# Rotary exchange of a head's halves: ScalarE copies between partitions instead of a permutation product

## The chip, the cores and the metric

The kernel runs on one core of one Trainium2 chip. The metric is the device time of one execution in microseconds (us). Names used below: PE is TensorE's matmul, PEld its weight load, DVE VectorE, ACT ScalarE, POOL GpSimd, SP SyncE, which issues most DMAs.

## The reference

Two stacks of layers on 256 tokens of width 1024, all in float32. The first has a recurrent mixer, an attention and two feed-forward layers. The second begins with a projection into q, k, v of two attentions (`m` and `d`) and their gates; q and k get a rotary embedding; then come the attentions, the output product, the routing and 32 experts. Cut to the part at stake:

```python
def apply_rope(x, cos, sin):
    xf = x.astype(jnp.float32)
    half = x.shape[-1] // 2
    x1, x2 = xf[..., :half], xf[..., half:]
    return jnp.concatenate([x1 * cos - x2 * sin, x2 * cos + x1 * sin], axis=-1).astype(x.dtype)

q_m, k_m, v_m, q_d, k_d, v_d, gate_m, gate_d = jnp.split(proj, IN_SPLITS, axis=-1)
qm = apply_rope(to_heads(q_m, MOBA_HEADS, MOBA_HEAD_DIM), cos_m, sin_m)
km = apply_rope(to_heads(k_m, MOBA_HEADS, MOBA_HEAD_DIM), cos_m, sin_m)
qd = apply_rope(to_heads(q_d, 2 * DIFF_HEADS, DIFF_HEAD_DIM), cos_d, sin_d)
kd = apply_rope(to_heads(k_d, 2 * DIFF_HEADS, DIFF_HEAD_DIM), cos_d, sin_d)
```

## The kernel before

Features lie on partitions and tokens along the free axis, so that a head of 64 features is 64 partitions and a tile of 128 partitions holds two heads. The exchange of a head's halves is therefore a movement between partitions: 0-31 with 32-63, 64-95 with 96-127.

**Stages.** Each engine runs a program of its own, written in order by hand; semaphores join them. The stage at stake starts when the feed-forward of the second layer ends and lasts until the attention scores. The weights come in units of 2 MB, named qm, km, vm, qd, kd, vd, gm0 and so on, through three places in SBUF (`RING`). Each product is made of three float32r products of a high and a low part of both operands. For every unit, ACT rounds the weights to the high part in two halves (`hi_unit`, line 715) and DVE subtracts to get the low part in two halves (`lo_unit`, line 1097); PE waits for both parts (`wait_parts`) before the unit's first tile.

**Tiles.** PE makes each unit in two tiles (km0, km1, ...), each in a PSUM bank: `product_pair_parts` (line 1766), `product_pair_rows` for km0 (line 1778), `token_major_parts` for the v units (line 1787). Banks 0 to 3 go round by the order of the list `TILES`; `start_tile` waits until the tile four places earlier has been read out (`evac`). ACT reads a finished tile out with `copy_pair` (line 694). The q of `m` is made apart (`qm_product`, line 2007) and finished in SBUF by `qm_shifted`.

**Rotation.** `rotate` (line 2028) multiplies the tile in SBUF with a 128x128 matrix `rot` of -1 and 1, plain float32, in 4 places of PE's program: for qm behind tile km0, for km behind vm0, for qd behind kd0, for kd behind vd0. Each place has two tiles rot0 to rot7 of two products. DVE then does, for each of the eight (r = 0 to 7), x * cos (line 1417), the exchanged x from PSUM * sin (line 1418), both in two pieces of 256 columns, and their sum (line 1421). In DVE's program, `lo_unit` of qd stands ahead of r = 2, kd behind r = 3, vd ahead of r = 4, gm0 behind r = 7.

**After it.** `pair_scores(0)` (lines 2059, 2062) waits for all eight rotated tiles and for the last read-outs; then come gate products (`gate_tile`, line 2076), the softmax on DVE (from line 1440) and ACT, and later the experts, whose weights SP loads as PE frees the places.

Of the kernel before, what the change touches and what calls it, by code (L numbers as in the profile page):

```python
# [25 lines left out]
P = 128  # L26
# [26 lines left out]
C_ID, C_AFTER, C_BEFORE, C_ONES, C_ROT, C_STICK, C_NEG = 0, 128, 256, 384, 512, 640, 1024  # L53
C_IOTA = 1408
# [31 lines left out]
         + ["km0", "rot0", "rot1", "km1", "vm0", "rot2", "rot3", "vm1",  # L86
            "qd0", "qd1", "kd0", "rot4", "rot5", "kd1", "vd0", "rot6", "rot7", "vd1"]
# [40 lines left out]
def program(nc, a, mod_dram, out):  # L128
    with ExitStack() as ctx:
# [41 lines left out]
        rot = cst[:, C_ROT:C_ROT + P]  # L171
# [49 lines left out]
        rope_u = flat(TMP + 1024, 512)  # L221
        ada_place = [wbuf[:, at:at + UNIT // 2].rearrange("p (j f) -> p j f", j=ADA_GROUP) for at in (6 * MATRIX + UNIT, 6 * MATRIX + UNIT + UNIT // 2)]
# [62 lines left out]
        def col(row, table=0):  # L285
# [28 lines left out]
        ffn_g, ffn_gu, ffn_silu, ffn_hid, ffn_hid_hi, ffn_hid_lo = (  # L314
            sem(n) for n in ("ffn_g", "ffn_gu", "ffn_silu", "ffn_hid", "ffn_hid_hi", "ffn_hid_lo"))
# [13 lines left out]
        mean_ready = sem("mean_ready")  # L329
        merged_ready = sem("merged_ready")  # L330
# [175 lines left out]
        def _(sp):  # L506
# [43 lines left out]
            sp.dma_start(cst[:, C_ROT:], a["constants"][:, C_ROT:]).then_inc(const_in, 16)  # L550
# [119 lines left out]
        def _(act):  # L670
# [166 lines left out]

            act.add_instruction(mybir.InstLoadActFuncSet(name=nc.get_next_instruction_name(), act_func_set_id=EXP_LN_TABLE, ins=[], outs=[]))
# [71 lines left out]
            copy_pair("km0", km[:, 0:2])  # L910
            copy_pair("km1", km[:, 2:4])
# [145 lines left out]
        def _(dve):  # L1057
# [212 lines left out]
            def ffn(layer):  # L1270
# [7 lines left out]
                def step(s, n, following=True):  # L1278
# [12 lines left out]
                    dve.wait_ge(ffn_hid, 2 * n + 1)  # L1291
                    dve.wait_ge(ffn_silu, n + 1)
                    nc.vector.tensor_tensor(hid[:, s], hid[:, s], up_scaled, ALU.mult).then_inc(ffn_hid, 1)
                    dve.wait_ge(ffn_hid, 2 * n + 2)
                    nc.vector.tensor_copy(hid_part[s][0], hid[:, s]).then_inc(ffn_hid_hi, 1)
                    subtract(hid_part[s][1], hid[:, s], hid_part[s][0], ffn_hid_hi, n + 1, ffn_hid_lo)
# [110 lines left out]
            for i, x in enumerate((qm, km, qd, kd)):  # L1407
# [314 lines left out]
        def _(pe):  # L1722
# [288 lines left out]
            def second_product(nm, h):  # L2011
# [4 lines left out]
                else:  # L2016
                    product_pair_parts(f"{nm}{h}", unit_parts(nm), 2 * h, KC, x_part)

            def rotate(nm, x, r):

                for d in range(2):
                    if nm == "qm":
# [349 lines left out]
```

## Time and profile before

| what | value |
|---|---|
| time, median of 3 runs | 1292.6 us (1289.51 to 1292.88) |
| the profiled execution's own time | 1292.79 us |
| its span in the trace | 1291.0 us |
| PE busy | 1120.0 us, 87% |
| DVE busy | 685.0 us, 53% |
| ACT busy | 420.7 us, 33% |
| granted TensorE clock, mean | 0.952 |

The span is the time from the first to the last instruction in the trace; the 1.8 us between it and the execution's time lie around it. Shares of busy time are means over stages with different limits, so the stretch from 636 to 715 us is read by itself: the chain of waits says what the end hung on, the timelines of PE, ACT and DVE say when each started what, and the brackets behind a row how long the engine had been idle and who ended that.

### The profile page before, as it was taken

How to read it: one execution, taken by the hardware profiler on the slowest of the kernel's cores; microseconds unless marked ns; L12 is line 12 of the kernel's file. 1: busy time of each engine (PE TensorE's matmuls, PEld its weight loads, DVE VectorE, ACT ScalarE, POOL GpSimd, SP SyncE). 2: the span in 40 equal slices, each digit the busy share in tenths (PEclk: the TensorE clock that was granted, in tenths of full speed). 3: DMA queues.
4: the chain of work that ended last, by engine and by line, in shares of the span. 5: the costliest groups of instructions: out<-in, count | busy, mean ns of one | idle time of the engine just before them, and what ended most of it. 6: DMA issues, size and time to landing. Idle time of an engine off the chain costs nothing.

```text
span 1291.0 us, 23141 instructions
## 1 busy us (share of the span) xinstructions
PE 1120.0 (87%) x9332; PEld 907.3 (70%) x9333; DVE 685.0 (53%) x1069; ACT 420.7 (33%) x532; POOL 32.7 (3%) x71
## 2 busy tenths in 40 slices
PE   9999999999989999999999999768666667666666
PEld 9999999999968999999998899633232223222222
DVE  5799888887444565556866777532211212112114
ACT  3775333345474333335644673320000000000001
POOL 0000000000000000001000000000000000000000
PEclk9999999999999999999999998899988889888889
DMA  9678988865520965551463335889999999999996
GB/s 349 218 272 303 326 304 302 305 239 189 175 94 1 350 208 170 166 180 34 156 244 131 131 139 210 328 330 409 428 429 429 427 429 428 428 428 429 429 427 255
DMA packets 99401, 362.48 MB, mean 281 GB/s; under 512 B 4160, under 2 KB 51664, under 8 KB 84112
## 3 DMA queue, kind: packets, MB, share of 16 engines
q1 hardware_dynamic: 95216, 335.06, 67.3%
q0 software_dynamic: 3984, 26.50, 5.2%
q8 instruction: 43, 0.70, 0.2%
q14 instruction: 14, 0.11, 0.0%
q10 hardware_dynamic: 144, 0.10, 0.0%
HBM read 360.58 MB, written 1.06 MB: 280 GB/s over the span
## 4 chain that ended last, share of the span: by engine, by line
PE 58%; DMA 24%; DVE 11%; ACT 3%; issue 3%; SPq 1%; POOLq 0%; DVEq 0%; POOL 0%; ACTq 0%
DMA wbuf<-in_w_up 22%; PE ps L1880 16%; PE ps L1803 9%; PE ps L1766 8%; PE ps L2200 6%; DVE parts L1097 3%; PE ps L1787 3%; PE ps L2076 3%; PE ps L1812 2%; PE ps L2220 1%; PE ps L2250 1%; DMA wbuf<-in_ffn_w_in 1%; PE ps L1756 1%; PE ps L1963 1%; DVE wbuf L1175 1%
## 5 line engine op out<-in xcount | busy, mean ns | idle before, releaser
L2200 PE MATMUL ps<-wbuf,big 128*32 128x256 f32 x2176 | 164.6, 467 | 112.4 <-DMA wbuf<-in_w_up 98.4
L1880 PE MATMUL ps<-big_parts,parts 128*128 128x256 f32 x2112 | 257.7, 283 | 4.8 <-DVE parts L1097 4.8
L1880 PEld LDWEIGHTS ps<-big_parts,parts 128*128 128x128 f32 x2112 | 254.9, 190 | 5.8 <-DVE parts L1097 5.8
L1097 DVE TENSOR_TENSOR parts<-wbuf,parts 128x2048 fp32r<-128x2048 f32 x92 | 208.8, 2287 | 88.6 <-ACT parts L829 45.2
L2200 PEld LDWEIGHTS ps<-wbuf,big 128*32 128x32 f32 x2176 | 83.6, 133 | 206.9 <-issue 105.3
L1676 DVE TENSOR_TENSOR big<-big,ps 128x128 f32<-128x128 f32 x33 | 9.5, 288 | 266.5 <-ACT big L1029 266.5
L1029 ACT ACTIVATE big<-ps 128x128 f32<-128x128 f32 x33 | 9.1, 277 | 417.0 <-PE ps L2200 417.0
L1803 PE MATMUL ps<-big_parts,parts 128*128 128x256 f32 x1152 | 142.0, 282 | 1.7 <-DVE parts_f L1347 1.1
L1803 PEld LDWEIGHTS ps<-big_parts,parts 128*128 128x128 f32 x1152 | 139.3, 189 | 2.1 <-issue 1.3
L1766 PE MATMUL ps<-parts_f,parts 128*128 128x256 f32 x704 | 98.4, 284 | 0.0
L1766 PEld LDWEIGHTS ps<-parts_f,parts 128*128 128x128 f32 x704 | 90.5, 192 | 0.1
L2250 PE MATMUL ps<-wbuf,big 128*32 128x512 f32 x544 | 65.4, 596 | 16.2 <-DVE big L1664 16.2
L1097 DVE TENSOR_TENSOR parts<-wbuf,parts_f 128x2048 fp32r<-128x2048 f32 x28 | 63.3, 2288 | 17.7 <-ACT parts_f L715 17.6
L2220 PE MATMUL ps<-big 64*128 64x512 f32 x272 | 67.6, 615 | 2.6 <-DVE big L1672 2.6
L734 ACT ACTIVATE parts<-wbuf 128x2048 fp32r<-128x2048 f32 x22 | 42.1, 1916 | 83.6 <-PE ps L1880 60.0
L715 ACT ACTIVATE parts<-wbuf 128x2048 fp32r<-128x2048 f32 x26 | 48.4, 1905 | 33.1 <-PE ps L1766 18.1
L829 ACT ACTIVATE parts<-wbuf 128x2048 fp32r<-128x2048 f32 x20 | 38.3, 1913 | 63.9 <-PE ps L1803 63.9
L1175 DVE SCALAR_TENSOR_TENSOR wbuf<-wbuf,big 128x1024 f32<-128x1024 f32 x48 | 56.0, 1220 | 0.3 <-DMA wbuf<-in_w_ada 0.3
L737 ACT ACTIVATE parts<-wbuf 128x2048 fp32r<-128x2048 f32 x22 | 42.2, 1916 | 40.5 <-PE ps L1880 36.6
L715 ACT ACTIVATE parts_f<-wbuf 128x2048 fp32r<-128x2048 f32 x28 | 52.4, 1903 | 3.3 <-PE ps L1766 3.3
L2076 PE MATMUL ps<-parts_f 128*128 128x256 f32 x256 | 47.1, 286 | 1.3 <-DVE parts L1097 1.3
L2220 PEld LDWEIGHTS ps<-big 64*128 64x128 f32 x272 | 23.4, 186 | 34.1 <-issue 32.4
(349 smaller groups left out, 1397.8 us busy)
## 6 DMA issues: line engine op xcount, KB each, us to landing
wbuf<-in_w_down SPq DMA_DIRECT2D x32, 2048.0 KB, 37.9
wbuf<-in_w_gate SPq DMA_DIRECT2D x31, 2048.0 KB, 32.6
wbuf<-in_w_up SPq DMA_DIRECT2D x31, 2048.0 KB, 37.1
wbuf<-in_ffn_w_in SPq DMA_DIRECT2D x44, 1024.0 KB, 11.7
wbuf<-in_w_ada POOLq DMA_DIRECT2D x24, 1024.0 KB, 8.6
wbuf<-in_ffn_w_out SPq DMA_DIRECT2D x22, 1024.0 KB, 5.1
wbuf<-in_w_in SPq DMA_DIRECT2D x10, 2048.0 KB, 8.2
wbuf<-in_attn_w_qkv SPq DMA_DIRECT2D x6, 2048.0 KB, 8.6
```

The lines of the kernel that those rows point to most:

```text
L715: nc.scalar.activation(halves(unit_parts(name)[0])[i], halves(unit_view(name))[i], ACT.Copy).then_inc(w_hi, 1)
L734: nc.scalar.activation(fg_part[0], ffn_views(slot)[0], ACT.Copy).then_inc(fg_hi, 1)
L737: nc.scalar.activation(fu_part[0], ffn_views(slot)[1], ACT.Copy).then_inc(fu_hi, 1)
L1097: nc.vector.tensor_tensor(lo, whole, hi.bitcast(F32), ALU.subtract).then_inc(done, 1)
L1175: ins = nc.vector.scalar_tensor_tensor(out=w, in0=w, scalar=1.0, in1=c_row, op0=ALU.mult, op1=ALU.mult, accum_out=ada[:, at:at + 1])
L1766: ins = mm(b[:, d * 256:(d + 1) * 256], w[pw][:, k, (m + d) * P:(m + d + 1) * P], rhs[px][:, k], start=(k == 0 and i == 0), stop=(k == kn ...
L1803: ins = mm(ps[:, 4 + f // 2, (f % 2) * 256:(f % 2 + 1) * 256], w[:, k, f * P:(f + 1) * P], r, start=(first and k == 0 and f % 2 == 0), sto ...
L1880: ins = mm(ps[:, b, d * 256:(d + 1) * 256], w[pw][:, k, d * P:(d + 1) * P], h_part_of[px][:, k], start=(k == 0 and d == 0 and i == 0), sto ...
L2076: ins = mm(ps[:, c % 2, d * 256:(d + 1) * 256], w[pw][:, k, m * P:(m + 1) * P], x_part[px][:, k], start=(k == 0 and i == 0), stop=(k == KC ...
L2200: ins = mm(at, rows, gu_place[s][:, :, k, r * P:(r + 1) * P], start=(k == 0), stop=(k == KC - 1))
L2220: ins = mm(ps[:, 4 + 2 * c + h, :], comb[q][rows, c * P:(c + 1) * P], yE[q][rows, :], start=False, stop=stop, skip_group_check=True)
L2250: ins = mm(ps[r * WIN:(r + 1) * WIN, 2, :], hidT[:, f * WIN:(f + 1) * WIN], d_place[s][:, f, h * 512:(h + 1) * 512], start=(i == 0), stop= ...
```

## The change

The product with `rot` goes, with its matrix in the constants (905 columns loaded become 777) and the tiles rot0 to rot7. In its place ACT copies each quarter of 32 partitions to its partner's place, 4 copies of 32x512 for each of the 8 pairs of tiles' columns, into one of two SBUF buffers `swapped`; the sign moves into the sine table. DVE now works on 512 columns at once, three operations for each r. A semaphore of the feed-forward is merged with its neighbour (same waits; a register operation more in each turn of a loop of four turns, twice).

```diff
-         + ["km0", "rot0", "rot1", "km1", "vm0", "rot2", "rot3", "vm1",
-            "qd0", "qd1", "kd0", "rot4", "rot5", "kd1", "vd0", "rot6", "rot7", "vd1"]
+         + [f"{nm}{i}" for nm in ("km", "vm", "qd", "kd", "vd") for i in range(2)]
...
+        swapped = [flat(WORK + 6144 + 512 * i, 512).rearrange("p (k t) -> p k t", k=2) for i in range(2)]
...
+            def swap_halves(r, of):
+
+                if r >= 2:
+                    act.wait_ge(roped, r - 1)
+                for h in range(P // HD):
+                    for to, at in ((0, HD // 2), (HD // 2, 0)):
+                        ins = nc.scalar.activation(swapped[r % 2][h * HD + to:h * HD + to + HD // 2], of[h * HD + at:h * HD + at + HD // 2], ACT.Copy)
+                ins.then_inc(swap_done, 1)
+
+            def copy_swapped(name, dst, r):
+                wait_tile(act, name)
+                swap_halves(r, bank(name).rearrange("p (k t) -> p k t", k=2))
+                copy_pair(name, dst)
...
             hi_unit("vm")
-            copy_pair("km0", km[:, 0:2])
-            copy_pair("km1", km[:, 2:4])
+            for h in range(2):
+                act.wait_ge(qm_kept, 2 * h + 2)
+                swap_halves(h, qm[:, 2 * h:2 * h + 2])
+            copy_swapped("km0", km[:, 0:2], 2)
+            copy_swapped("km1", km[:, 2:4], 3)
             hi_unit("qd")
             copy_pair("vm0", vm[:, 0])
             copy_pair("vm1", vm[:, 1])
             hi_unit("kd")
-            copy_pair("qd0", qd[:, 0:2])
-            copy_pair("qd1", qd[:, 2:4])
+            copy_swapped("qd0", qd[:, 0:2], 4)
+            copy_swapped("qd1", qd[:, 2:4], 5)
             hi_unit("vd")
-            copy_pair("kd0", kd[:, 0:2])
-            copy_pair("kd1", kd[:, 2:4])
+            copy_swapped("kd0", kd[:, 0:2], 6)
+            copy_swapped("kd1", kd[:, 2:4], 7)
             hi_unit("gm0")
...
-                    wait_tile(dve, f"rot{r}")
-                    for kk in range(2):
-                        nc.vector.tensor_tensor(t3[:, kk], xx[:, kk], rope[:, 0:256], ALU.mult)
-                        ins = nc.vector.tensor_tensor(u3[:, kk], bank(f"rot{r}")[:, kk * 256:(kk + 1) * 256], rope[:, 256:512], ALU.mult)
-                    ins.then_inc(evac_sem(f"rot{r}"), 1)
-                    wait_evac(dve, f"rot{r}")
+                    if nm == "qm":
+                        dve.wait_ge(qm_kept, 2 * d + 2)
+                    else:
+                        wait_evac(dve, f"{nm}{d}")
+                    nc.vector.tensor_tensor(t3, xx, cosine, ALU.mult)
+                    dve.wait_ge(swap_done, r + 1)
+                    link(nc.vector.tensor_tensor(u3, swapped[r % 2], sine, ALU.mult))
                     ins = nc.vector.tensor_tensor(xx, t3, u3, ALU.add)
...
             product_pair_rows("km0", unit_parts("km"), 0, KC, x_part, FH_MOD)
-            rotate("qm", qm, 0)
             second_product("km", 1)
             second_product("vm", 0)
-            rotate("km", km, 2)
             second_product("vm", 1)
             for h in range(2):
                 second_product("qd", h)
             second_product("kd", 0)
-            rotate("qd", qd, 4)
             second_product("kd", 1)
             second_product("vd", 0)
-            rotate("kd", kd, 6)
             second_product("vd", 1)
```

ACT's program before, from the high part of vm on: the read-outs of km (line 694) stand between the high parts of vm and of qd.

```order
L715 ACTIVATE parts_f<-wbuf 128x2048 [waits fu_lo,a_loaded0]
L715 ACTIVATE parts_f<-wbuf 128x2048
L694 ACTIVATE big<-ps 128x512 [waits tile_done] x2
L715 ACTIVATE parts_f<-wbuf 128x2048 [waits tile_done,a_loaded1]
L715 ACTIVATE parts_f<-wbuf 128x2048
```

The same place now, where line 844 is the copy of a quarter:

```order
L715 ACTIVATE parts_f<-wbuf 128x2048 [waits fu_lo,a_loaded0]
L715 ACTIVATE parts_f<-wbuf 128x2048
L844 ACTIVATE big<-big 32x512 [waits qm_kept]
L844 ACTIVATE big<-big 32x512 x3
L844 ACTIVATE big<-big 32x512 [waits qm_kept]
L844 ACTIVATE big<-big 32x512 x3
L844 ACTIVATE big<-ps 32x512 [waits roped,tile_done]
L844 ACTIVATE big<-ps 32x512 x3
L694 ACTIVATE big<-ps 128x512 [waits tile_done]
L844 ACTIVATE big<-ps 32x512 [waits roped,tile_done]
L844 ACTIVATE big<-ps 32x512 x3
L694 ACTIVATE big<-ps 128x512 [waits tile_done]
L715 ACTIVATE parts_f<-wbuf 128x2048 [waits tile_done,a_loaded1]
```

Sixteen copies stand between the two high parts, and eight of them wait for DVE's rotated tiles (`roped`).

PE's program before, at the end of tile km0 (line 1778) and the start of km1 (line 1766):

```order
L1778 MATMUL ps<-parts_f,parts 128x256
L2028 MATMUL ps<-big,cst 128x256 [waits evac1,qm_kept]
L2028 MATMUL ps<-big,cst 128x256
L2028 MATMUL ps<-big,cst 128x256 [waits evac2,qm_kept]
L2028 MATMUL ps<-big,cst 128x256
L1766 MATMUL ps<-parts_f 128x256 [waits evac3]
```

The same place now, where the lines are 1797 and 1785:

```order
L1797 MATMUL ps<-parts_f 128x256 x2
L1797 MATMUL ps<-parts_f,parts 128x256
L1785 MATMUL ps<-parts_f 128x256 [waits evac1]
L1785 MATMUL ps<-parts_f 128x256
```

The four products are gone and km1 goes into bank 1 instead of 3; the other three places change in the same way.

DVE's program now, from the low part of vm (line 1114, before 1097) to that of qd; lines 1437, 1439 and 1440 are the two multiplications and the sum:

```order
L1114 TENSOR_TENSOR parts<-wbuf,parts_f 128x2048 [waits w_hi] x2
L1437 TENSOR_TENSOR big<-big 128x512 [waits qm_kept,rope_in]
L1439 TENSOR_TENSOR big<-big 128x512 [waits swap_done]
L1440 TENSOR_TENSOR big<-big 128x512 [waits dve_ch]
L1437 TENSOR_TENSOR big<-big 128x512 [waits qm_kept,roped]
L1114 TENSOR_TENSOR parts<-wbuf,parts_f 128x2048 [waits w_hi,roped]
```

Every r is now three operations, and the second waits for ACT (`swap_done`) where the first waited for PE's tile.

## Rows read from the trace of the kernel before

**Rows 1.** The page's head: span and instructions

```profile
span 1291.0 us, 23141 instructions
```

**Rows 2.** Chain of waits, 590 to 740 us: start us, us, what

```profile
638.12 1.73 PE ps L2028 x8
...
645.60 5.47 PE ps L1787 x24
...
658.24 17.27 PE ps L1766 x144
...
688.46 0.88 PE ps L2028 x4
...
698.79 0.57 DVE big L1440
...
714.51 6.01 PE ps L2076 x48
```

**Rows 3.** PE's timeline: start us, us, engine, line, shapes, count [idle before <-releaser]

```profile
645.43 0.63 PE L1787 MATMUL ps<-parts_f 128*128 128x512 f32 x2
...
658.08 0.40 PE L1766 MATMUL ps<-parts_f 128*128 128x256 f32 x2
...
696.42 0.49 PE L2059 MATMUL ps<-big 64*128 64x128 f32 x4 [0.78 <-ACT big L694]
...
698.36 0.51 PE L2076 MATMUL ps<-parts_f 128*128 128x256 f32 x2 [1.01 <-DVE parts L1097]
...
714.51 0.50 PE L2076 MATMUL ps<-parts_f 128*128 128x256 f32 x2 [0.26 <-DVE parts L1097]
```

**Rows 4.** ACT's timeline, 605 to 725 us

```profile
638.46 3.70 ACT L715 ACTIVATE parts_f<-wbuf 128x2048 fp32r<-128x2048 f32 x2
642.07 0.57 ACT L694 ACTIVATE big<-ps 128x512 f32<-128x512 f32 x1
...
658.28 0.60 ACT L694 ACTIVATE big<-ps 128x512 f32<-128x512 f32 x1 [6.58 <-PE ps L1787]
658.77 3.71 ACT L715 ACTIVATE parts_f<-wbuf 128x2048 fp32r<-128x2048 f32 x2
```

**Rows 5.** DVE's timeline, 605 to 725 us

```profile
608.87 0.69 DVE L1293 TENSOR_TENSOR big<-big 128x512 f32<-128x512 f32 x1
...
640.55 4.49 DVE L1097 TENSOR_TENSOR parts<-wbuf,parts_f 128x2048 fp32r<-128x2048 f32 x2
644.96 0.41 DVE L1417 TENSOR_TENSOR big<-big 128x256 f32<-128x256 f32 x1
...
646.41 0.69 DVE L1421 TENSOR_TENSOR big<-big 128x512 f32<-128x512 f32 x1
647.13 0.43 DVE L1417 TENSOR_TENSOR big<-big 128x256 f32<-128x256 f32 x1
...
660.78 4.49 DVE L1097 TENSOR_TENSOR parts<-wbuf,parts_f 128x2048 fp32r<-128x2048 f32 x2 [2.72 <-ACT parts_f L715]
```

**Rows 6.** ACT's groups by form: busy us, mean ns | idle before

```profile
L798 ACT ACTIVATE big<-xT 128x512 f32<-128x512 f32 x16 | 9.9, 616 | 0.0
L1029 ACT ACTIVATE big<-ps 128x128 f32<-128x128 f32 x33 | 9.1, 277 | 417.0 <-PE ps L2200 417.0
...
L694 ACT ACTIVATE big<-ps 128x512 f32<-128x512 f32 x10 | 5.9, 595 | 33.9 <-PE ps L1766 18.2 <-PE ps L1787 15.7
```

**Rows 7.** PE's timeline behind four waits

```profile
453.06 13.25 PE L1880 MATMUL ps<-big_parts,parts 128*128 128x256 f32 x96 [2.85 <-DVE parts L1097]
...
919.51 3.66 PE L2200 MATMUL ps<-wbuf,big 128*32 128x256 f32 x64 [2.64 <-DMA wbuf<-in_w_up]
...
948.90 5.35 PE L2200 MATMUL ps<-wbuf,big 128*32 128x256 f32 x64 [4.00 <-DMA wbuf<-in_w_up]
...
1227.83 3.66 PE L2200 MATMUL ps<-wbuf,big 128*32 128x256 f32 x64 [3.58 <-DMA wbuf<-in_w_up]
```

**Rows 8.** Stretches: us, PE busy (x), granted clock, DMA share, GB/s

```profile
454.00:457.80 3.80, 3.80 (x22) 0.56 0.48 153
...
949.00:952.50 3.50, 3.50 (x40) 0.55 1.01 431
```

**Rows 9.** Waits of SP's queue: us in total, times, longest

```profile
SPq L497 <- PE ps L2200: 234.4, 27, 20.7
...
SPq L594 <- DVE info L1646: 22.6, 1, 22.6
```

More of the change, by code:

```diff
@@ L313, in program @@
         ffn_gate_scaled = sem("ffn_gate_scaled")
-        ffn_g, ffn_gu, ffn_silu, ffn_hid, ffn_hid_hi, ffn_hid_lo = (
-            sem(n) for n in ("ffn_g", "ffn_gu", "ffn_silu", "ffn_hid", "ffn_hid_hi", "ffn_hid_lo"))
+        ffn_g, ffn_gu, ffn_silu, ffn_hid, ffn_hid_lo = (
+            sem(n) for n in ("ffn_g", "ffn_gu", "ffn_silu", "ffn_hid", "ffn_hid_lo"))
         fh_hi, fh_lo, fg_hi, fg_lo, fu_hi, fu_lo, fd_hi, fd_lo = (
@@ L549, in _ @@
             sp.dma_start(cst[:, 0:C_ONES], a["constants"][:, 0:C_ONES]).then_inc(const_in, 16)
[L550 removed]
+            sp.dma_start(cst[:, C_STICK:], a["constants"][:, C_STICK:]).then_inc(const_in, 16)
             sp.dma_start(bias36[:], a["rows"][:, 0:N_GRP + N_EXP].to_broadcast([P, N_GRP + N_EXP])).then_inc(lam_in, 16)
@@ L1406, in _ @@
             dve.wait_ge(rope_in, 16)
-            for i, x in enumerate((qm, km, qd, kd)):
+            cosine, sine = (rope[:, SEQ * i:SEQ * (i + 1)].unsqueeze(1).to_broadcast([P, 2, SEQ]) for i in range(2))
+            for i, (nm, x) in enumerate((("qm", qm), ("km", km), ("qd", qd), ("kd", kd))):
                 for d in range(2):
@@ L2017, in second_product @@
                     product_pair_parts(f"{nm}{h}", unit_parts(nm), 2 * h, KC, x_part)
-            def rotate(nm, x, r):
-                for d in range(2):
-                    if nm == "qm":
-                        pe.wait_ge(qm_kept, 2 * d + 2)
-                    else:
-                        wait_evac(pe, f"{nm}{d}")
-                    b = start_tile(f"rot{r + d}")
-                    for kk in range(2):
-                        ins = mm(b[:, kk * 256:(kk + 1) * 256], rot, x[:, 2 * d + kk], start=True, stop=True)
-                    ins.then_inc(tile_done, 1)
             wait_parts("qm")
@@ L2312, in constant_arrays @@
     half = HD // 2
-    for o in range(P):
-        if o % HD < half:
-            table[o + half, C_ROT + o] = -1.0
-        else:
-            table[o - half, C_ROT + o] = 1.0
     table[:, C_STICK:C_STICK + P] = np.where(i[:, None] >= i[None, :], NEG, 0.0)
@@ L2326, in constant_arrays @@
     ang = ang[i % half]
-    rope = np.concatenate([np.cos(ang), np.sin(ang)], axis=1).astype(np.float32)
+    sign = np.where(i % HD < half, -1.0, 1.0)[:, None]
+    rope = np.concatenate([np.cos(ang), sign * np.sin(ang)], axis=1).astype(np.float32)
     slots = np.broadcast_to(np.arange(SLOTS, dtype=np.float32), (P, SLOTS)).copy()
```

14 lines of the change are left out of this document (7 added, 7 removed).

## The prediction

> **What bounds the kernel now.** I took the page's head first [rows 1], then the chain of waits, then the timelines of PE, ACT and DVE over the stretch that the change touches, then the waits of SP's queue. In the chain [rows 2] the reader is to see that from 638 us to the end of the v products every piece is PE's: the rotation for qm takes 1.73 us, a v tile 5.47, three q or k tiles in a row 17.27, which is 5.76 each. There are four rotation pieces; three are 1.73 and the last is there with 0.88, since the chain leaves PE in its middle for DVE. In PE's own timeline it takes its full time ahead of tile vd1. PE is without a gap here: the first vm product starts at 645.43 and the first of qd at 658.08 [rows 3]. Only at the exit do others decide: the scores wait 0.78 us for the last read-out and start at 696.42; the first gate product waits 1.01 more, for the low part of gm0, and starts at 698.36 [rows 3]; the softmax starts on DVE at 698.79 [rows 2]. The third gate product, at 714.51, waited only 0.26 for DVE [rows 3]; PE and DVE arrive there together, and behind it PE is the chain again [rows 2]. In the expert stage SP waits for PE 27 times before it loads, and once 22.6 us for the routing's result before the fourth expert [rows 9]: what is won ahead of it starts the stream of weights earlier and is kept.
>
> **The change part by part.**
>
> *Removed from PE.* 4 x 1.73 = 6.9 us of products [rows 2], all on the path. The question is whether the weights' parts, which ACT and DVE make, come as much earlier. They don't, at two places.
>
> *vm.* The low part of vm ends on DVE at 640.55 + 4.49 = 645.04 [rows 5], and nothing in front of it changes. PE would now be there at 645.43 - 1.73 = 643.7 and waits until 645.1. That is a wait of 1.4 us; the two tiles then end at 645.1 + 2 x 5.47 = 656.0 [rows 2, 3].
>
> *The copies on ACT.* Thirty-two copies of 32x512 are added. No row shows 32 partitions or a shift between partitions. The nearest rows are the copies of 128x512: 616 ns from SBUF and 595 ns from PSUM [rows 6], and as they stand behind one another 0.49 from start to start (658.28 to 658.77) from PSUM [rows 4]. I take 0.50 from PSUM and 0.52 from SBUF, by the length and not by the number of partitions. The bounds: 0.28, if a quarter of the partitions cost as a quarter of the length does (128x128, 277 ns [rows 6]); and 1.0, twice the row, if reading at one place and writing at another can't go together. The Trainium skill (page "ScalarE: Activation LUTs", section "What ACT_TABLE_LOAD costs") gives a copy of 128 partitions 186 ns + 0.833 ns per element, with 93 ns of overlap between neighbours: 0.52 us each, as an estimate from that page, for PSUM too; that would add 8 x 0.02 = 0.16 us ahead of qd. The page counts nothing by partitions, which speaks against this change, as four quarters then cost four whole copies; no row here tests it.
>
> *qd.* ACT is done with the high part of vm and starts its next at 642.07 [rows 4]. The copies r = 0, 1 take 8 x 0.52: to 646.2. The buffers are two, so r = 2 waits for DVE's sum of r = 0. DVE starts that at 644.96 [rows 5]; 128x512 takes 0.61 before an independent one and 0.69 + 0.02 before a dependent one [rows 5], so an r costs 0.61 + 0.72 + 0.72 = 2.05, against 647.13 - 644.96 = 2.17 before [rows 5]; the first sum ends at 647.0. Then r = 2: 4 x 0.50 and the read-out of km0 0.50 to 649.5; r = 3 the same to 652.0 (DVE's second sum, at 649.1, is in time). The high part of qd thus starts at 652.0. The low part starts 2.01 behind the high part's start (658.77 to 660.78 [rows 4, 5]) and lasts 4.49: done at 658.5, and PE starts qd0 at 658.6. It would have been there at 656.0: a wait of 2.6 us. Compared with 658.08 before, qd0 is 0.5 us **later**, although two rotations are gone.
>
> *kd, vd, gm0.* From here PE runs at its own pace. The high part of kd starts behind vm1's read-out at 656.7, DVE's r = 2, 3 end at 662.6, its low part of kd at 667.1, needed at 658.6 + 2 x 5.76 = 670.1. qd1 ends there; r = 5 and its read-out end at 672.7, high vd starts, low vd is done at 672.7 + 2.01 + 4.49 = 679.2, needed at 681.6. Then r = 4, 5 end on DVE at 683.3, and ACT's copies for r = 6, which wait for r = 4, run from 681.2; r = 7 and its read-out end at 686.2; DVE's r = 7 at 688.4, low gm0 at 692.9. All that is hidden, by 2.4 to 3 us, gm0 by less: 28 copies lie on its way (16 ahead of qd, 4 for r = 5, 8 for r = 6 and 7) against 16 on PE's, and if each costs over about 0.6, gm0 is the last at the exit.
>
> *Exit.* PE's last tile ended at 696.42 - 0.78 = 695.64 [rows 3]. Now 695.64 + 0.5 - 2 x 1.73 = 692.7, scores at 693.5. Low gm0 (692.9) no longer holds the first gate product: it starts when the scores are issued, 0.93 behind their start (698.36 - 1.01 - 696.42 [rows 3]), at 694.4, 3.9 us earlier. The softmax starts at about 694.3, 4.5 earlier than 698.79 [rows 2]. At the third gate product PE arrives at 714.51 - 0.26 - 3.9 = 710.3 and DVE's low part no later, so 4.2 us are won [rows 3].
>
> *The clock.* A wait can cost more than itself. Behind a wait of 4.00 us 64 expert products took 5.35 us, and behind waits of 2.64 and 3.58 us 3.66 [rows 7]; the granted clock behind the first was 0.55 [rows 8], that is mostly the lower level, 1.2 GHz. Behind a wait of 2.85 us of an else fully busy PE it was 0.56 for 3.8 us [rows 7, 8]. So a wait of 2.6 us, with another of 1.4 some 11 us earlier, lies where it goes either way, and a fall costs 5.35 - 3.66 = 1.7 us. All that follows on ACT and DVE waits for qd's tiles, so it passes on in full. I take the fall as the likelier, as the row with a busy PE is the nearest: 4.2 - 1.7 = **2.5 us** won. The Trainium skill (page "TensorE: Matmul & The Clock Gate", section "Loop structure matters more than you think") calls a wait for data between bursts what makes TensorE go cold; by that rule the new wait costs the 1.7 us, without it the sum is 4.2.
>
> *At nothing.* The merged semaphore adds 8 register operations to DVE's queue in a loop whose chain is PE's; the 64 KB less of constants come in while the chain is on PE. DVE's shorter r (8 x 0.12) lies where PE is the chain. SP's order is the same; kd is loaded sooner, as its place is free 1.7 us earlier.
>
> Sum for the profiled execution: 1292.8 - 2.5 = 1290.3, which stands 0.2 above the median of 1292.6, so for the median **1290.1 us**.
>
> **The rivals.**
>
> *A: no fall of the clock.* The same waits, the price left out: 1292.6 - 4.2 = 1288.4. For it: 3.58 us without one [rows 7]. The times would lie in two groups if it changes from one execution to the next. If the copies cost 0.28, ACT would start qd's high part 1.3 us sooner (647.0 + 2 x (4 x 0.28 + 0.50) = 650.2, but r = 3 waits for DVE's 649.1, so 650.7), and 1287.1 results.
>
> *B: slower, since the copies are dear.* Up to qd sixteen copies lie in a row on ACT's path. At 1.0 each, r = 1 ends at 650.1, r = 3 and its read-out at 659.1, low qd at 665.6: qd0 is 7.5 us later than before instead of 0.5. At the exit ACT's r = 6, 7 then run from DVE's r = 4 at about 692 to 701, low gm0 ends near 707.4, 9.1 us later than 698.3; with the clock's 1.7 that is 1303.4. It decides where the 28 copies on gm0's way eat the 2.5 us and the 0.9 by which gm0 is early for the softmax (694.3 against 692.9 and three small steps of 0.5): (2.5 + 0.9) / 28 = 0.12 more than taken, at 0.62 a copy. For it: no row shows the operation. Against it: every form of copy in the trace goes by its length.
>
> *C: all of PE's time is won.* If the parts of qd came in time, 4.2 + 2.6 = 6.8 are won: 1285.8. Against it: ACT's order alone, sixteen copies ahead of qd, for which even 0.28 is too long.
>
> *D: the gain is lost later.* The expert stage is fed by DMA; if the stream of weights did not start earlier, the time stays 1292.6. Against it: SP waits for PE and the routing there [rows 9].
>
> **How the numbers follow.** Forecast (wait and fall) 0.48, A 0.25, B 0.12, C 0.05, D 0.10. A measurement of this kernel can tell about 0.3% from no change, here 3.9 us, so the border is 1288.7. The forecast's own range is 1288.5 to 1292. The whole: 1286.5 holds A and its cheap copies, 1295.5 reaches into B up to copies of 0.5 + (5.4 + 0.9) / 28 = 0.72; outside lie C and most of B. Faster by over 0.3%: two thirds of A and more (0.18), C (0.05), the lower edge of the forecast (0.07), 0.30. Slower: nearly all of B (0.11) and a mishap not named (0.02), 0.13. Within: 0.57.
>
> **What would show it.** No L2028 rows; PE idle 1.4 us ahead of the first vm product, released by DVE, and 2.6 ahead of the first qd product, also by DVE's low part; the granted clock near 0.5 for some 3 us behind that; 32 copies at 0.50 from start to start; the third gate product near 712.0 (710.3 without a fall). Wrong if PE waits elsewhere (kd, vd or gm0), if a copy's step is not within 0.45 to 0.6, or if the gain at 714 is not that of the end.

## The result and the profile after

The changed kernel takes 1293.7 us (median of 20 runs, 1291.96 to 1296.96), the kernel before on the same chip 1291.6 (1288.76 to 1295.45): a ratio of 1.0018, 95% interval 1.0010 to 1.0026. It is **slower by 0.18%, some 2.3 us**, where 2.5 us less were forecast. (All ratios and intervals here come from all runs of the two kernels in the same comparison; they need not be the quotient of the medians.) The result lies within the 0.3% given as no change and inside the range of 1286.5 to 1295.5, but the sign was wrong, and the interval shows it.

The profiled execution of the changed kernel took 1293.78 us. The page's head, to be set against [rows 1]:

```profile
span 1292.0 us, 23098 instructions
```

PE's timeline, against [rows 3]: start us, us, engine, line, shapes, count, and in brackets the idle time before and who ended it.

```profile
646.48 0.74 PE L1806 MATMUL ps<-parts_f 128*128 128x512 f32 x2 [1.23 <-DVE parts L1114]
...
661.38 0.51 PE L1785 MATMUL ps<-parts_f 128*128 128x256 f32 x2 [3.69 <-DVE parts L1114]
...
697.84 0.49 PE L2062 MATMUL ps<-big 64*128 64x128 f32 x4 [0.78 <-ACT big L694]
...
698.81 0.50 PE L2079 MATMUL ps<-parts_f 128*128 128x256 f32 x2
...
714.95 0.50 PE L2079 MATMUL ps<-parts_f 128*128 128x256 f32 x2 [0.25 <-DVE parts L1114]
```

The rotation's products are gone, and PE waits at the two places that were named: 1.23 us ahead of vm (1.4 forecast) and 3.69 ahead of qd (2.6 forecast). Absolute times need a common point. I take the start of DVE's low part of vm, behind which the change begins: 640.55 before [rows 5], 641.94 here. From there to the third gate product it was 73.96 us [rows 3, 5] and is now 714.95 - 641.94 = 73.01. The stretch of the rotation gained 0.95 us, not 2.5.

ACT's timeline (line 844 is the copy between quarters, 694 the read-out, 715 the high part), against [rows 4]:

```profile
643.57 5.13 ACT L844 ACTIVATE big<-big 32x512 f32<-32x512 f32 x8
648.73 2.40 ACT L844 ACTIVATE big<-ps 32x512 f32<-32x512 f32 x4
651.15 0.60 ACT L694 ACTIVATE big<-ps 128x512 f32<-128x512 f32 x1
651.78 2.39 ACT L844 ACTIVATE big<-ps 32x512 f32<-32x512 f32 x4
654.19 0.60 ACT L694 ACTIVATE big<-ps 128x512 f32<-128x512 f32 x1
654.82 3.72 ACT L715 ACTIVATE parts_f<-wbuf 128x2048 fp32r<-128x2048 f32 x2
658.44 1.06 ACT L694 ACTIVATE big<-ps 128x512 f32<-128x512 f32 x2
```

A quarter costs what a whole copy does: 5.13 / 8 = 0.64 from SBUF and 2.40 / 4 = 0.60 from PSUM. The last row has two whole read-outs in 1.06, so the second one starts before the first has ended; the quarters and the read-outs behind them stand end to start. The sixteen copies and two read-outs that stand ahead of qd's high part take 654.82 - 643.57 = 11.25 us. By the forecast they ended 11.45 us behind the common point; they end 12.88 behind it.

DVE's timeline, against [rows 5]. The rotation on 512 columns costs what was forecast, 648.39 - 646.34 = 2.05 an r, and low qd waits for ACT:

```profile
641.94 4.49 DVE L1114 TENSOR_TENSOR parts<-wbuf,parts_f 128x2048 fp32r<-128x2048 f32 x2
646.34 0.69 DVE L1437 TENSOR_TENSOR big<-big 128x512 f32<-128x512 f32 x1
...
648.39 0.69 DVE L1437 TENSOR_TENSOR big<-big 128x512 f32<-128x512 f32 x1
...
656.84 4.49 DVE L1114 TENSOR_TENSOR parts<-wbuf,parts_f 128x2048 fp32r<-128x2048 f32 x2 [6.43 <-ACT parts_f L715]
```

The chain of waits, against [rows 2], shows the same from the end backwards. Before, PE's tiles held it without a break; now it runs through ACT's copies, DVE's low part and one block of PE, and through ACT and DVE again to the softmax (line 1459):

```profile
651.15 0.60 ACT big L694
...
654.82 1.93 ACT parts_f L715
656.84 4.50 DVE parts L1114 x2
661.38 13.27 PE ps L1785 x96
...
691.50 0.61 ACT big L694
...
694.26 4.49 DVE parts L1114 x2
699.24 0.57 DVE big L1459
```

The low part of gm0 is the last thing ahead of the softmax, as was said for copies of more than about 0.6 us.

The stretch does not explain a slower kernel. The other half is 550 us further on, in the last expert. First PE's timeline of the changed kernel, then that of before:

```profile
1267.78 2.35 PE L2203 MATMUL ps<-wbuf,big 128*32 128x256 f32 x37 [0.18 <-issue]
1273.15 3.60 PE L2203 MATMUL ps<-wbuf,big 128*32 128x256 f32 x27 [3.02 <-issue]
```

```profile
1271.95 3.83 PE L2200 MATMUL ps<-wbuf,big 128*32 128x256 f32 x64
```

The same 64 products take 3.83 us before and 3.60 + 1273.15 - 1267.78 = 8.97 now: PE stops for 3.02 us after the 37th, and the other 27 take 3.60 us where 37 took 2.35. The stretches of time (us, busy time and count of PE and the other engines, granted clock, DMA share, GB/s) give the lower level, 1.2 GHz, for those 27, as for the products behind the wait at qd:

```profile
662.30:665.60 3.30, 3.30 (x17) 3.30 (x17) 3.16 (x6) 0.80 (x1) 0.00 (x0) 0.50 0.80 301
...
1273.50:1276.50 3.00, 3.00 (x27) 1.13 (x19) 0.00 (x0) 0.00 (x0) 0.00 (x0) 0.50 0.01 3
```

Behind these 64 products the two traces are alike again: 1292.01 - 1276.75 = 15.26 us to the end of the changed kernel's, 1291.02 - 1275.78 = 15.24 before. Until the last expert the changed kernel was ahead: it began it 4.17 us earlier (1267.78 against 1271.95). The stop is no wait for data: it is put down to "issue", the last expert's semaphores are waited for every 16 products, and the 37th stands in the middle of such a group. The DMA view of the stop, 1270.2 to 1273.1 us, shows a piece of program coming in on q8 (packets, MB, share of the 16 DMA engines' time). That the piece is PE's is inferred from its time and not shown:

```profile
q1 hardware_dynamic: 142, 0.63, 54.6%
q8 instruction: 1, 0.02, 2.2%
```

Between 915 and 1269 us no packet is on q8: the experts before the last run in a loop, and the last one is written out behind it. The whole run has 43 packets on q8, 0.70 MB in all, so 16 KB each. The change takes 72 instructions out of PE's program (the rotation's 64 matmuls and weight loads, and 8 on semaphores), so all code behind it stands 72 places earlier.

### The profile page after: what moved, and what is told of

Its sections match the earlier page's. It is cut to its first block, busy times and chain, and to the rows that moved or that the text cites. A ratio compares the mean times of both kernels' runs of the same rounds, so it can differ in the third digit from the quotient of the medians.

```text
span 1292.0 us, 23098 instructions
## 1 busy us (share of the span) xinstructions
PE 1115.8 (86%) x9299; PEld 900.7 (70%) x9301; DVE 683.9 (53%) x1053; ACT 439.8 (34%) x564; POOL 32.6 (3%) x71
## 3 DMA queue, kind: packets, MB, share of 16 engines
HBM read 360.52 MB, written 1.06 MB: 280 GB/s over the span
## 4 chain that ended last, share of the span: by engine, by line
PE 54%; DMA 24%; DVE 12%; ACT 6%; issue 3%; SPq 1%; another core or an unknown queue 1%; POOLq 0%; DVEq 0%; POOL 0%; ACTq 0%
DMA wbuf<-in_w_up 22%; PE ps L1899 15%; PE ps L1822 9%; PE ps L1785 7%; PE ps L2203 6%; DVE parts L1114 4%; PE ps L2079 3%; PE ps L1831 2%; PE ps L1806 2%; PE ps L2223 1%; PE ps L2253 1%; ACT parts_f L715 1%; DMA wbuf<-in_ffn_w_in 1%; ACT big L844 1%; PE ps L1775 1%
## 5 line engine op out<-in xcount | busy, mean ns | idle before, releaser
L2203 PE MATMUL ps<-wbuf,big 128*32 128x256 f32 x2176 | 167.9, 473 | 111.5 <-DMA wbuf<-in_w_up 97.0
```

The lines of the kernel that those rows point to most:

```text
L2203: ins = mm(at, rows, gu_place[s][:, :, k, r * P:(r + 1) * P], start=(k == 0), stop=(k == KC - 1))
```

## The experiments

**Is it the place of the code? First try, with padding.** Both kernels get instructions that only add to a semaphore, ahead of the routing product for which PE waits: 72 in the changed kernel, which puts the last expert back, and 184 in the one before.

```diff
+            for _ in range(72):            # 184 in the kernel before
+                nc.tensor.nop().then_inc(ones_ready, 1)
             pe.wait_ge(logit_read, 1)
```

> The changed kernel with 72 empty semaphore instructions in PE's program, put where PE waits 6.6 us for the routing; with them everything behind stands at the same place of PE's instruction stream as in the kernel before. Theory 1 (part of the loss is the place at which PE's instructions are fetched: the changed kernel idles 3.0 us in the middle of the last expert's gate product at 1270 us, with an instruction fetch at 1270.7, and runs on at the lower clock): that idle goes, the clock stays up, and the time falls by about 3 to 5 us against the changed kernel, to about 1289. Rival (the idle is an accident of one execution or belongs to the weights' DMA): the same time as the changed kernel, 1293.7, with the idle where it was or in some executions only.

> The kernel before with 184 empty semaphore instructions in PE's program at the same wait; 184 and not 72 fewer, as a fetch brings 256 instructions, so the code behind stands in a fetch as in the changed kernel. Theory 1: an idle of about 3 us appears in the last expert's gate product, behind an instruction fetch, and the time rises by 3 to 5 us, to about 1295. Rival (accident, or caused by the changed stage): no idle there and the time of before, 1291.5; 184 instructions of about 20 ns are 4 us and fit in the 6.6 us wait.

Measured: the changed kernel with 72 takes 1293.44 us, ratio 1.0026 (1.0013 to 1.0038), where about 1289 was expected; the kernel before with 184 takes 1315.04, ratio 1.0196 (1.0180 to 1.0211), where about 1295 was. The padding itself was dear. PE's idle time ahead of the routing product was 6.61 us before; with 72 and with 184 it is

```profile
830.83 0.21 PE L2176 MATMUL ps<-rstd_half 128*128 128x64 bf16 x1 [10.49 <-issue]
```

```profile
850.50 0.21 PE L2173 MATMUL ps<-rstd_half 128*128 128x64 bf16 x1 [27.84 <-issue]
```

so one of them takes (27.84 - 10.49) / (184 - 72) = 0.155 us and not the 20 ns expected, and the totals say little. The last expert says more: its products are whole in the padded changed kernel, and broken in the padded kernel before (rows of the one, then of the other):

```profile
1272.62 3.81 PE L2205 MATMUL ps<-wbuf,big 128*32 128x256 f32 x64
```

```profile
1290.65 2.35 PE L2202 MATMUL ps<-wbuf,big 128*32 128x256 f32 x37 [0.18 <-issue]
1296.03 3.18 PE L2202 MATMUL ps<-wbuf,big 128*32 128x256 f32 x27 [3.03 <-issue]
```

72 fewer and 184 more differ by 256, and both break behind the 37th product. If the pattern repeats with 256 instructions and a piece holds as many, 16 KB would be 64 bytes an instruction, an estimate from the two. The two places fit a repeat of 128 or 64 as well; no run tells them apart.

**Second try, the place without the cost.** PE starts with 20 plain float32 products of 128 columns as a warm-up. Two of 512 columns in the kernel before are 72 instructions fewer; 38 of 64 columns in the changed one are 72 more. The same was done to a kernel with three steps of ACT and DVE in another order (below).

```diff
-WARM_UP = 20
+WARM_UP = 2                       # the other two: 38, of 64 columns
-                mm(ps[:, 6, 0:P], ones, ones, start=True, stop=True)
+                mm(ps[:, 6, 0:512], ones, ones[:, 0:1].to_broadcast([P, 512]), start=True, stop=True)
```

> The kernel before with a warm-up of 2 plain float32 products of 512 columns in place of 20 of 128: 72 PE instructions fewer, so that its last expert's code stands where the changed kernel's does; nothing of the rotation is touched. The warm-up takes about 3.1 us instead of 7.6, so the start can move by -4.5 (PE was the last there) to +2 (lower clock for the first products), and is read apart. Theory 1 (place of the code): an idle of 2.5 to 3.1 us in the last expert's 64 gate and up products and the lower clock behind it, length 7.5 to 9.0 instead of 3.8; the time from the first expert to the end grows by 3.5 to 5. Theory 2 (something that only the changed kernel does): length 3.8, no idle.

> The changed kernel with the warm-up of 38 products of 64 columns, 72 PE instructions more and nothing else. Theory 1 (place of the code): no idle in the last expert's products, length 3.8 instead of 9.0; the gain of 1 us in the stretch of the rotation is all that is left of the change: 0.9980 to 0.9995 of before, against 1.0018 for the changed kernel. Theory 2 (timing): the idle stays and the time is 1.0018 again. If the fall at the rotation and nothing else cost the change its gain, this kernel would not move either.

> The kernel of the three altered places, and PE's warm-up ahead of the first product made of 38 plain float32 products of 64 columns in place of 20 of 128: about the same time there, and 72 PE instructions more, so that PE's code behind the rotation stands where it stood before the change. Theory 1 (the idle of 3 us in the last expert's products and the lower clock behind it come from where PE's code stands against the pieces in which it is fetched): no idle over 1 us in the last 64 gate and up products, their length 3.8 instead of 7.5 to 9.0, and the time 3.5 to 5 us under that of the kernel without the longer warm-up: 0.995 to 0.996 of before. Theory 2 (the idle comes from the DMA traffic or the timing of the changed kernel, not from the length of its code): the idle stays, the time is within 0.5 of the kernel without it, 0.998 to 0.999.

Measured: the kernel before with 72 fewer takes 1295.21, ratio 1.0040 (1.0026 to 1.0055). Nothing of the rotation is touched in it, and it now has the stop and the lower clock, with 3.55 us for the last 27 products:

```profile
1268.80 2.35 PE L2200 MATMUL ps<-wbuf,big 128*32 128x256 f32 x37 [0.24 <-issue]
1274.35 3.55 PE L2200 MATMUL ps<-wbuf,big 128*32 128x256 f32 x27 [3.20 <-issue]
```

The two with 72 more have whole last experts (3.78 and 3.74 us), but 1299.63 and 1294.66 in total, ratios 1.0072 and 1.0033: both totals are misses of mine. The short products don't go by their columns; the warm-up took 16.47 us instead of 7.64:

```profile
1.15 16.47 PE L1842 MATMUL ps<-cst 128*128 128x64 f32 x76 [1.15 <-DVE cst L1096]
```

**Third try, with a cheap warm-up and its control.** 76 bfloat16 products of 128 columns are 72 instructions more as well; 40 of them in the kernel before leave its length as it is.

```diff
-WARM_UP = 20
+WARM_UP = 76                      # 40 in the kernel before
-                mm(ps[:, 6, 0:P], ones, ones, start=True, stop=True)
+                nc.tensor.matmul(ps[:, 6, 0:P], ones.bitcast(mybir.dt.bfloat16)[:, 0:P], ones.bitcast(mybir.dt.bfloat16)[:, 0:P], start=True, stop=True)
```

> The changed kernel with the same warm-up of 76 bfloat16 products and nothing else, 72 PE instructions more: what the change is worth when PE's code behind the rotation stands where it stood before. Theory 1: last expert's products 3.8 us instead of 9.0, the gain of 1 us at the third gate product is left, 0.998 to 0.9995 of before where the changed kernel had 1.0018. Theory 2 (the change itself costs the time, by its copies): 1.001 to 1.003 as before.

> The control for the warm-up alone: the kernel before with 40 bfloat16 products of 128 columns in place of 20 float32 ones, 80 PE instructions as before, so nothing behind it changes its place. Theory 1 and 2 both: last expert's products 3.8 us; the start moves by -4 to 0 us (40 of them take 3.5 to 5 us, then PE waits until about 6.8 for the first weights, and runs its first products at the lower clock, as with the two long products), and the time is 0.999 to 1.001 of before. If it is faster by over 1.5 us, the two kernels beside it owe that much to their warm-up and not to their place.

Measured, side by side: the changed kernel with 76 products 1288.54, ratio 0.9993 (0.9984 to 1.0002); the control 1291.30, ratio 0.9998 (0.9986 to 1.0010). Without the 76 products the changed kernel had 1.0018 (1.0010 to 1.0026), in the comparison of the result, and the intervals with and without the 72 don't meet. In the control the new warm-up makes no difference beyond 0.14%. The place is thus worth 0.25%, 3.2 us, with 0.13 to 0.37% as an estimate of the interval from the two. The last expert is whole:

```profile
1267.67 3.73 PE L2203 MATMUL ps<-wbuf,big 128*32 128x256 f32 x64
```

Its stretch from the common point to the third gate product is 73.02 us, as in the changed kernel, and it waits 3.72 us at qd. What the change is worth by itself in the whole time is thus 0.07% less, 0.9 us, with an interval from 0.16% less to 0.02% more, so no gain is not excluded. (The medians, 1288.54 and 1290.67 for the kernel before, lie further apart, 2.1 us; its 11 runs spread from 1287.60 to 1291.55.) The stretch is the sharper measure: 73.96, 73.98 and 73.95 us in the kernel before, in the one with 72 fewer and in the control, 73.01 and 73.02 in the changed kernel and this one.

The place measured in two more pairs comes out larger: 0.42% (5.4 us) from the control's 0.9998 to the 1.0040 of the kernel before with 72 fewer, and 0.33% (4.3 us) from 0.9986 to 0.9953 in the reordered kernels below. The three agree within their intervals. In the traces of the changed kernel and of before the last expert's products alone differ by 8.97 - 3.83 = 5.14 us, but the experts ahead of it tended to take less where the stop is: from the first expert's products to the last one's 431.0 to 432.6 us in the five traces with the stop (the two kernels with other copies, below, left out), 432.2 to 435.1 in the seven without. Whether the place causes that too is not shown.

**Why did the stretch give only 0.95? ACT's order at qd.** In the changed kernel ACT makes qd's high part ahead of the eight copies and two read-outs for km, not behind them.

```diff
             for h in range(2):
                 act.wait_ge(qm_kept, 2 * h + 2)
                 swap_halves(h, qm[:, 2 * h:2 * h + 2])
+            hi_unit("qd")
             copy_swapped("km0", km[:, 0:2], 2)
             copy_swapped("km1", km[:, 2:4], 3)
-            hi_unit("qd")
```

> The changed kernel with ACT's high part of qd moved ahead of the read-outs and copies of km. Theory 2 (the sixteen copies ahead of qd cost 0.64 and 0.60 us each instead of 0.52 and 0.50, and with them PE waits 3.7 us for qd and falls to the lower clock): the wait ahead of the first qd product goes, only the 1.2 to 1.4 us ahead of vm stays, the clock stays up, and the first gate product starts 3.7 + 1.7 = 5.4 us earlier relative to the start of the stage, less what gm0 holds back (about 1 us). The time falls by 4 us against the changed kernel, to about 1289.5. Rival (PE is then held at kd, vd or gm0 instead): less than 1 us won in the stage, a new wait of PE ahead of one of these.

Measured: 1288.31, ratio 0.9989 (0.9980 to 0.9999), though its last expert is broken as well (7.51 us). From ACT's timeline and DVE's:

```profile
641.38 5.13 ACT L844 ACTIVATE big<-big 32x512 f32<-32x512 f32 x8
646.54 3.72 ACT L715 ACTIVATE parts_f<-wbuf 128x2048 fp32r<-128x2048 f32 x2
```

```profile
639.75 4.49 DVE L1114 TENSOR_TENSOR parts<-wbuf,parts_f 128x2048 fp32r<-128x2048 f32 x2
...
648.56 4.49 DVE L1114 TENSOR_TENSOR parts<-wbuf,parts_f 128x2048 fp32r<-128x2048 f32 x2 [0.34 <-ACT parts_f L715]
```

Low qd is ready at 648.56 + 4.49 = 653.05, and PE has no wait at qd and no fall of the clock: 646 to 667 us is one stretch at full speed (the granted clock is the next to last but one number):

```profile
646.00:667.00 21.00, 21.00 (x140) 19.37 (x139) 15.11 (x14) 17.69 (x22) 0.00 (x0) 1.00 0.67 248
```

The third gate product starts at

```profile
707.32 0.50 PE L2079 MATMUL ps<-parts_f 128*128 128x256 f32 x2 [0.24 <-DVE parts L1114]
```

so the stretch takes 707.32 - 639.75 = 67.57 us, 5.44 less than in the changed kernel: the wait of 3.69, and 1.75 that are left for the fall of the clock, 1.7 by the forecast. It is 6.4 less than before. PE's 6.9 less the 1.23 at vm, and with the wait of 1.01 for gm0's low part at the exit [rows 3] gone, would be 6.7; the other 0.3 stay open.

**gm0's parts ahead too.** ACT's high part of gm0 goes ahead of the copies for kd, and DVE's low part ahead of r = 6.

```diff
+            hi_unit("gm0")
             copy_swapped("kd0", kd[:, 0:2], 6)
             copy_swapped("kd1", kd[:, 2:4], 7)
-            hi_unit("gm0")
...
-                    if d == 0 and i in (1, 2):
-                        lo_unit(("qd", "vd")[i - 1])
+                    if d == 0 and i in (1, 2, 3):
+                        lo_unit(("qd", "vd", "gm0")[i - 1])
```

> The changed kernel with three places of order altered and nothing else: ACT makes the high part of qd ahead of its copies for km0 and km1, and the high part of gm0 ahead of those for kd0 and kd1; DVE makes the low part of gm0 ahead of the products for r = 6 and 7. Where only qd's high part was moved, the stretch from vm's low part to the third gate product took 67.6 us instead of 73.0. Theory 1 (what remains of the loss at the exit is gm0's low part, last ahead of the softmax): low gm0 ends several us before the scores, the stretch takes 66 to 67.5, and the time is 0 to 1 us under that of the kernel with qd alone, 0.9980 to 0.9990 of before. Theory 2 (the exit is PE's own by then; gm0 was late only since everything was): 67.4 to 67.8, no change against the qd kernel, 0.9989. Both: the last expert's gate and up products are still interrupted by an idle of 2.5 to 3 us, since PE's program is as long as in the changed kernel.

Measured: 1288.52, ratio 0.9986 (0.9974 to 0.9998), the stretch 67.58 us: no gain over the kernel with qd alone. The last expert has its stop, as expected (3.34 us). Theory 2 holds; once qd is in time, gm0's low part no longer sets the exit.

**The version that beats both.** This kernel with the 76 bfloat16 products:

> The kernel with qd's and gm0's parts moved ahead, and a warm-up of 76 bfloat16 products of 128 columns in place of 20 plain float32 ones: a product in bfloat16 is two PE instructions where a float32 one is four, so there are again 72 more. The 38 float32 products of 64 columns took 16.5 us, 8.8 more than the 20, and hid what the place of the code gives; 76 of these should take 7 to 10 us, as an estimate from the f32r products of 256 columns at 0.123 each. Theory 1 (place of the code): last expert's 64 products 3.8 us instead of 9.3, and 0.9940 to 0.9965 of before. Theory 2 (the loss is given back elsewhere, as the stream of weights sets the end): 0.998 to 0.999, as without it.

Measured: 1284.34, ratio 0.9953 (0.9938 to 0.9969), 0.47% or 6.1 us less than before, where the stretch has won 6.4. The stretch is 67.58 us and the last expert whole:

```profile
1263.78 3.81 PE L2201 MATMUL ps<-wbuf,big 128*32 128x256 f32 x64
```

**Why 0.60 and 0.64 a copy?** Two kernels with other copies in place of these (the rotated values are not the reference's, so their times count for nothing, and only their rows are read). In the first, r = 1 and 4 are four straight quarters, r = 3 and 5 spread one quarter over all four, r = 6 crosses them in another order:

```diff
+                straight = ((0, 0), (32, 32), (64, 64), (96, 96))
+                crossed = ((0, 32), (32, 0), (64, 96), (96, 64))
+                pieces = {1: straight, 3: ((0, 32), (32, 32), (64, 32), (96, 32)), 4: straight,
+                          5: ((0, 0), (32, 0), (64, 0), (96, 0)), 6: ((0, 32), (64, 96), (32, 0), (96, 64))}.get(r, crossed)
```

> The changed kernel with other patterns of the four quarters in some of the eight exchanges, so the rotated values are not the reference's: r = 0, 2, 7 crossed as in the changed kernel; r = 1, 4 straight (each quarter to its own place); r = 3 and r = 5 one source quarter to all four places; r = 6 the crossed pairs in another order. Theory 2a (a copy that starts at another partition than its neighbour cannot overlap with it, whether crossed or not): all of them 0.64 from SBUF and 0.60 from PSUM from start to start. Rival 2b (the crossing costs it): r = 1 and 4 take 0.52 and 0.50. Rival 2c (only the reader's or only the writer's change of partition matters): r = 3 and 5, where the source stays, differ from r = 4.

```profile
647.89 2.40 ACT L847 ACTIVATE big<-ps 32x512 f32<-32x512 f32 x4
...
650.94 2.39 ACT L847 ACTIVATE big<-ps 32x512 f32<-32x512 f32 x4
...
667.97 2.39 ACT L847 ACTIVATE big<-ps 32x512 f32<-32x512 f32 x4 [5.71 <-PE ps L1788]
```

These are r = 2, crossed, r = 3, spread, and r = 4, straight: no difference. So the shift between partitions costs nothing, and the loss of overlap has another cause. The second kernel:

```diff
+                crossed = ((0, 32), (32, 0), (64, 96), (96, 64))
+                places = [(k, t) for k in range(2) for t in range(2)]
+                whole = [(0, 0, P, k, t) for k, t in places]
+                corner = [(0, 0, 32, k, t) for k, t in places]
+                pieces = {0: whole, 1: whole, 2: [(to, at, 32, 0, 0) for to, at in crossed], 3: corner,
```

> The changed kernel with other copies by ACT in the eight places: for r = 0, 1 and 6 four copies of 128x128 (whole partitions, four groups of columns), for r = 3 four of 32x128 (partitions 0 to 31 each time, four groups of columns), for r = 2 four of 32x128 that cross the quarters, for r = 4 two of 64x512 straight, for r = 5 two of 64x512 crossed, r = 7 as in the changed kernel. The rotated values are not the reference's. The question is which property takes away the 0.1 us by which neighbouring 128x512 copies overlap (two from start to start 0.49, four quarters 0.60 each). Theory 1 (neighbours that start at different partitions don't overlap): r = 0, 1, 6 at 0.17 to 0.19 from start to start with 0.28 each, r = 3 the same, r = 2 at 0.26 to 0.28; r = 4 and 5 at 0.60. Theory 2 (copies of fewer than 128 partitions don't overlap): r = 3 at 0.26 to 0.28 as r = 2. Theory 3 (a copy of the rotation doesn't overlap, whatever its form, since its neighbours share a buffer): 128x128 at 0.27 too.

```profile
636.67 3.70 ACT L715 ACTIVATE parts_f<-wbuf 128x2048 fp32r<-128x2048 f32 x2
640.28 1.69 ACT L854 ACTIVATE big<-big 128x128 f32<-128x128 f32 x8
645.27 1.11 ACT L854 ACTIVATE big<-ps 32x128 f32<-32x128 f32 x4 [3.30 <-DVE big L1450]
...
647.34 0.74 ACT L854 ACTIVATE big<-ps 32x128 f32<-32x128 f32 x4 [0.32 <-DVE big L1450]
647.98 0.58 ACT L694 ACTIVATE big<-ps 128x512 f32<-128x512 f32 x1
...
661.06 1.20 ACT L851 ACTIVATE big<-ps 64x512 f32<-64x512 f32 x2 [2.30 <-PE ps L1795]
...
666.82 1.20 ACT L851 ACTIVATE big<-ps 64x512 f32<-64x512 f32 x2 [3.94 <-PE ps L1795]
```

Four 32x128 copies take 1.11 us when each is at another quarter and 0.74 when all are at quarter 0: 0.28 against 0.16 from start to start at 0.26 to 0.27 each. The read-out of 128 partitions at 647.98 overlaps the copy of 32 before it, and both start at partition 0; two 64x512 copies, one at 0 and one at 64, don't, straight (661.06) or crossed (666.82). Theories 2 and 3 fall with the 32x128 copies at quarter 0 and the 128x128 copies, and theory 1 stands: neighbours on ACT that start at different partitions lose the overlap of 0.1 us, whatever their number of partitions. A change of the written start alone is enough: r = 3 of the first kernel reads quarter 32 each time. A change of the read start alone goes with it too: the first crossed copy reads at 32 and writes at 0, as the high part of vm ahead of it does, and starts behind that one's end (643.57 against 639.84 + 3.71 in the changed kernel), where a 128x128 copy at the same place overlaps it (640.28 against 636.67 + 3.70). The other direction has an exception that I can't explain: in the changed kernel the read-out of km1 (654.19) and the high part of qd (654.82) both start at partition 0 and still stand end to start. The Trainium skill (page "ScalarE: Activation LUTs", section "What ACT_TABLE_LOAD costs") has the neighbours overlap by about 93 ns without such a condition; the rows agree with it at one start (but for that pair) and not across starts.

## Why the prediction was wrong, point by point

- **Removed products, 6.9 us, and the wait at vm**: right. The wait is 1.23 for 1.4, and with the wait at qd gone the stretch gains 73.96 - 67.57 = 6.4.
- **A copy at 0.50 and 0.52**: too small, 0.60 and 0.64. The rows read were of neighbours at one partition, 0.60 long and 0.49 apart. The eight from SBUF cost 0.96 more, but most of it went where a wait for DVE's first sum was foreseen: r = 2 starts 648.73 - 641.94 = 6.79 behind the common point for 6.45. The ten steps behind it, two read-outs among them, take 6.09 for 5.0. That makes 0.34 + 1.09 = 1.43, the delay of qd's high part; PE came there 0.3 later than forecast as well, and the wait grew from 2.6 to 3.69. By the prediction's own sign (a step outside 0.45 to 0.6) the 0.64 from SBUF was wrong. With the exit below this made the stretch's gain 0.95 for 2.5, a loss of 1.55.
- **Fall of the clock at qd**: right, 0.50 behind the wait; also after 3.72 in the kernel with the 76 products, where 661.0 to 664.4 had 0.62. Its price of 1.7 fits: 1.75 came back when qd was in time.
- **The exit**: the first gate product is 56.87 behind the common point, and by the forecast it was 694.4 + 1.7 - 640.55 = 55.55. gm0's low part is last ahead of the softmax, as said for over 0.6 a copy; but it is so only while qd is late.
- **The gain at 714 is that of the end**: wrong, and this step turned the sign. The gain itself did pass through the expert stage, so rival D falls: 6.4 us won in the stretch are 6.1 at the end (0.9953). What failed is the part **At nothing**, which had no term for PE's shorter program. The shorter program moved the last expert's code to a place where PE stops 3.02 us in the middle of its products and runs on at the lower clock. It cost 3.2 us (1.0018 against 0.9993), and that it is the place and not the rotation is shown from both sides: the kernel before shortened by 72 has the same stop, and the changed kernel lengthened by 72 has none.

Against the forecast of -2.5 us the result of +2.3 is thus 4.8 us off, 1.55 by the copies' price and 3.2 by the place of the code. That 0.9 less and 3.2 more give 2.3 more is no check, since the 3.2 is the difference of the other two; the check is that the 0.9 from the totals meets the 0.95 of the stretch. In the single profiled executions other stages moved too. The common point came 1.39 us later, but in kernels with the same code ahead of it it lies anywhere from 638.77 to 641.97. At 779 us the clock fell in the kernel before and not in the changed one (0.50 from 778.7 to 785.5 before, 1.00 after), and from the third gate product to the routing product it took 114.50 us before and 111.86 after. That is not the change's either: the control, unchanged, took 114.55 with the same fall, and the kernel before with 72 fewer 111.86 without one. The experts ahead of the last took 1.95 us less. So the changed kernel's lead of 4.17 us at the last expert is 0.95 from the stretch, 2.64 from that fall and 1.95 from the experts, less the 1.39; behind the stop's 5.14 its span is 1.0 us longer, 1292.0 against 1291.0.

Of the rivals B had the direction of the stretch's error (dearer copies, gm0 last at the exit) with too high a price: copies at 0.60 and 0.64 by themselves left a gain. A did not happen, the clock fell. C, with 6.8 us, is what the reordered kernel nearly reached. No rival named what turned the sign.

Open is what the stop consists of. The packet comes 0.56 us into it and takes 1.0, and PE goes on 1.4 us later; I can't say why it is not asked for sooner, nor why the piece of the kernel before, which comes at 1275.30 us and takes 1.0 as well, costs no stop.

## What to carry to other kernels

Count the instructions that an edit adds or removes on an engine, and look in both traces for a stop put down to "issue" inside a run of equal instructions, with an instruction packet in it: here the code written out behind a long loop paid 3 us and a fall of the clock, and a control with an equal number of instructions told that from the edit itself. Work handed to another engine goes behind what that engine makes for others: put the parts that the critical engine needs next ahead of it, which here was worth 5.4 us of the 6.4 won in the stretch. A step between neighbours read off the trace holds only for neighbours of the same kind; here the changing start partition made it 0.60 instead of 0.49.

## What the runs showed of the hardware that was not expected

- ACT copies from one quarter of the partitions to another in the time of a straight copy (2.40 and 2.39 us for four), and a quarter takes as long as the whole: 0.59 to 0.60 us for 32x512, 64x512 and 128x512 from PSUM.
- Two neighbours on ACT lose their overlap of 0.1 us when they start at different partitions (four 32x128 copies in 1.11 us across quarters, 0.74 at one).
- Where PE's code stands decides on a stop in it: 72 instructions fewer, or 184 more, break the same run of products behind the same one, the 37th, in all seven kernels that stand so (a stop of 2.3 to 3.3 us, and behind it the lower clock in five of them), and in none of the other seven. All of them are single traces.
- A PE instruction that only increments a semaphore takes 0.155 us in a row of them (27.84 and 10.49 us of idle time for 184 and 72), and a plain float32 product of 64 columns 16.47 / 76 = 0.217 for each of its two passes, where 128 columns take 7.64 / 40 = 0.191.
